# One transpose for the compressed probabilities of all heads of a step

## The chip, the cores and the metric

The kernel runs on one core of a Trainium2 chip. The metric is the time of one execution on the device, in microseconds (us), as the median of several runs. Five engines work side by side and meet at semaphores: TensorE (matmuls and transposes, into PSUM), VectorE and ScalarE (elementwise work and reductions, also out of PSUM), GpSimd (elementwise work in SBUF) and SyncE (here it issues the transfers from memory).

## The reference, cut to what matters

The whole program is two blocks over 256 tokens of width 1024. The first block has a retention layer, a sparse-attention layer and per-layer embeddings; the second has a gated delta rule, a forgetting attention and a feed-forward layer. The change lies in the sparse attention, in its compressed branch:

```python
s_c = jnp.einsum('bgrqd,bgnd->bgrqn', q, k_cmp).astype(jnp.float32) * scale
p_c = jnp.where(valid_c, jax.nn.softmax(jnp.where(valid_c, s_c, NEG), axis=-1), 0.0)
o_c = jnp.einsum('bgrqn,bgnd->bgrqd', p_c, v_cmp.astype(jnp.float32))
...
return gates[..., 0:1] * o_c + gates[..., 1:2] * o_s + gates[..., 2:3] * o_w
```

There are 16 heads in 4 groups of 4, a head is 128 wide, queries come in two blocks of 128, and there are 15 compressed keys (`CMP_N`) for each group. `v_cmp` is the result of a small two-layer network over windows of 32 tokens. With 256 tokens, the selected branch (`o_s`) and the window branch (`o_w`) are both plain causal attention.

## The kernel before, in words

All weights stream through a ring of four units of 1 MB (`ring`). ScalarE (L1461) writes each unit's high part, VectorE (L1855) what is left of it, and TensorE forms a product of two such numbers from three passes. Matmuls of plain float32 are two recorded passes each. Nearly every matmul of the program is recorded under the helper line L671.

PSUM has eight banks: four for projections and scores (`main`), four for the rest (`aux`). Each set is used in rotation in an order written out by hand. TensorE says when a bank is full, and the engine that reads it says when it is free again.

The compression network runs between the query projections. `turn_hidden` transposes its hidden values, VectorE copies them to `Pf` (L2038), `second_layer` makes the compressed keys and, in eight products, the compressed values (15 rows for each group, evicted at L2043).

The attention runs in 12 steps (`STEPS`): four with the four heads of a group for the first query block, then eight with two heads for the second. For step i:

- S: scores of the selected and the window branch; VectorE takes the maximum (L2060), ScalarE the exponential (L1627).
- N: VectorE makes the scales, GpSimd multiplies the probabilities by them (L2438).
- T (`nsa_turn`): TensorE transposes the probabilities, four times 128 x 128 for each branch (L1065), and the compressed ones, one 128 x 15 transpose for each head (L1071). VectorE copies the first (L2109), ScalarE the second (L1647), VectorE the compressed ones (L2111) to `nw`.
- O (`nsa_values`): the values' product of the three branches accumulates in one bank. The compressed one is first, contracts over 15 rows, and streams 128 columns for each head. VectorE multiplies the result by the gate (L2120); ScalarE (L1633) and VectorE (L1855) split it in two parts for the output projection.

The order on every engine is `nsa_order`: the scores of step i+2 stand between T and O of step i, and in the first three steps two gate projections stand there as well. Steps 10 and 11 have no scores left to put there.

`tab` holds constant tables: the identity (loaded first, by ScalarE's queue), masks, and tables of the second block (`TB_LEVEL`). All but the identity comes in one load, behind the first eight weight units in SyncE's queue. The tables `TB_STRICT` and `TB_INCL` aren't read.

Of the kernel before, what the change touches and what calls it, by code (L numbers as in the profile page):

```python
# [11 lines left out]
ALU = mybir.AluOpType  # L12
# [3 lines left out]
P = 128  # L16
# [91 lines left out]
SIDE_BG, SIDE_G2, SIDE_W2K, SIDE_W2V = 0, KD * 48, KD * 64, KD * 64 + 256  # L108
NSIDE = KD * 64 + 512

TB_ID, TB_CAUSAL, TB_CMP, TB_ROW, TB_STRICT, TB_INCL, TB_LEVEL = 0, 128, 256, 286, 288, 416, 544
TB_ONE = TB_LEVEL + 128 * len(LEVELS)
NTAB = TB_ONE + 15
RT_COS, RT_SIN, RT_DECAY = 0, 256, 512
# [2 lines left out]
def tables():  # L117

    i = np.arange(P)
    t = np.zeros((P, NTAB), np.float32)  # L120
    t[:, TB_ID:TB_ID + P] = np.eye(P)
    t[:, TB_CAUSAL:TB_CAUSAL + P] = np.where(i[None] <= i[:, None], 0.0, NEG)
    end = np.arange(CMP_N) * CMP_STRIDE + CMP_L - 1
    for b in range(TT):
        t[:, TB_CMP + b * CMP_N:TB_CMP + (b + 1) * CMP_N] = np.where(end[None] <= (b * P + i)[:, None], 0.0, NEG)
        t[:, TB_ROW + b] = (b * P + i >= CMP_L - 1)
    t[:, TB_STRICT:TB_STRICT + P] = np.where(i[None] < i[:, None], 0.0, -NEG)
    t[:, TB_INCL:TB_INCL + P] = np.where(i[None] >= i[:, None], 0.0, NEG)
    for n, m in enumerate(LEVELS):
        same = (i[:, None] // (2 * m)) == (i[None] // (2 * m))  # L130
        t[:, TB_LEVEL + n * P:TB_LEVEL + (n + 1) * P] = same & (i[:, None] // m % 2 == 1) & (i[None] // m % 2 == 0)
    t[:, TB_ONE + 7] = 1.0
    r = np.zeros((P, NRT), np.float32)
    inv = (np.float32(10000.0) ** (-np.arange(P, dtype=np.float32) / np.float32(P))).astype(np.float32)
    ang = (np.arange(T, dtype=np.float32)[None] * inv[:, None]).astype(np.float32)
    r[:, RT_COS:RT_COS + T] = np.cos(ang)
    r[:, RT_SIN:RT_SIN + T] = np.sin(ang)
    lg = np.log1p(-(2.0 ** (-5.0 - np.arange(RH))))
    diff = (np.arange(T)[None] - i[:, None]).astype(np.float64)
    for h in range(RH):  # L140
        r[:, RT_DECAY + h * T:RT_DECAY + (h + 1) * T] = np.where(
            diff >= 0, np.exp(np.maximum(diff, 0) * lg[h]), 0.0) * 256.0 ** -0.5
    return t, r
# [189 lines left out]
def two_models_kernel(nc, x, meta, weights, side, params, tabs, ret_tabs, p_t, gains, out):  # L333
    ctx = ExitStack()
    with ctx:
# [331 lines left out]
        def _(pe):  # L667
# [311 lines left out]
            def second_layer():  # L979

                wait_read(pe, aux, ("hT", 0))
                bank = aux.open(pe, ("c2", 0))
                for k in range(2):
                    ins = mm(bank[:, 0:CMP_ROWS], side_sb[:, SIDE_W2K + k * P:SIDE_W2K + (k + 1) * P],
                             Pf[:, k * CMP_ROWS:(k + 1) * CMP_ROWS], k == 0, k == 1)
                aux.full(ins, ("c2", 0))
                wait_read(pe, aux, ("hT", 1))
                bank = aux.open(pe, ("c2", 1))
                for g in range(NSA_G):
                    for k in range(2):  # L990
                        c0 = 2 * CMP_ROWS + k * CMP_ROWS + g * CMP_N
                        ins = mm(bank[0:CMP_N, g * P:(g + 1) * P], Pf[:, c0:c0 + CMP_N],
                                 side_sb[:, SIDE_W2V + k * P:SIDE_W2V + (k + 1) * P], k == 0, k == 1)
                aux.full(ins, ("c2", 1))

# [59 lines left out]
            def nsa_turn(i):  # L1055
                b, h0, nh = STEPS[i]
                kt = b + 1
                slot = i % 2

                pe.wait_ge(sem("nsa_p"), i + 1)  # L1060
                for key, base in ((("sT", i), 0), (("wT", i), 512)):
                    bank = aux.open(pe, key)
                    for n in range(4):
                        c0 = R2 + 2048 + slot * 1024 + base + n * P
                        ins = pe.transpose(bank[:, n * P:(n + 1) * P], R[:, c0:c0 + P], ident)  # L1065
                    aux.full(ins, key)
                pe.wait_ge(sem("cmp_p"), b + 1)
                bank = aux.open(pe, ("cT", i))
                for n in range(nh):
                    c0 = b * 240 + (h0 + n) * CMP_N  # L1070
                    ins = pe.transpose(bank[0:CMP_N, n * P:(n + 1) * P], xn[:, c0:c0 + CMP_N], ident)  # L1071
                aux.full(ins, ("cT", i))

            def nsa_values(i):
                b, h0, nh = STEPS[i]
                kt = b + 1
                slot = i % 2
                bank = aux.open(pe, ("o", i))
                for key in ("sT", "wT", "cT"):
                    wait_read(pe, aux, (key, i))  # L1080

                g = h0 // NSA_HPG
                o = bank[:, 0:nh * P]
                mm(o, Pf[0:CMP_N, CMP_V + g * P:CMP_V + (g + 1) * P], nw[0:CMP_N, slot * 512:slot * 512 + nh * P],
                   True, False)
                for br in range(2):
                    c0 = slot * 1024 + br * 512
                    p_t = PTb[:, c0:c0 + 512].rearrange("p (n k q) -> p k n q", n=nh, k=kt)
                    for k in range(kt):
                        v0 = R2 + br * 1024 + k * 512 + g * P  # L1090
                        ins = mm(o.rearrange("p (n q) -> p n q", n=nh), R[:, v0:v0 + P], p_t[:, k], False,
                                 br == 1 and k == kt - 1)
                aux.full(ins, ("o", i))
# [756 lines left out]
        def _(dve):  # L1850
# [184 lines left out]
            queries(6)  # L2035
            for n in range(2):
                bank = wait(aux, ("hT", n))
                aux.free(dve.tensor_copy(Pf[:, n * 120:(n + 1) * 120], bank[:, 0:120]), ("hT", n))  # L2038
            queries(7)
            bank = wait(aux, ("c2", 0))  # L2040
            aux.free(dve.tensor_scalar(Pf[:, CMP_K:CMP_K + CMP_ROWS], bank[:, 0:CMP_ROWS], 0.5, None, ALU.mult), ("c2", 0))
            bank = wait(aux, ("c2", 1))
            aux.free(dve.tensor_scalar(Pf[0:CMP_N, CMP_V:CMP_V + 512], bank[0:CMP_N, :], 0.5, None, ALU.mult), ("c2", 1))  # L2043
            after_read(main, ("bg", 1))
            own.then_wait(dve.tensor_scalar(bgt, bgt, 1.0, 0.5, ALU.add, ALU.mult))

# [7 lines left out]
            for kind, i in nsa_order():  # L2054
# [29 lines left out]
                elif kind == "N":  # L2084
                    b, h0, nh = STEPS[i]
                    after_read(main, ("w", i))
                    sc = esc[:, i * 8:i * 8 + 2 * nh]
                    own.then_wait(dve.reciprocal(sc, esum[:, i * 8:i * 8 + 2 * nh]))
                    g = bgt[:, b * 48 + h0 * 3:b * 48 + (h0 + nh) * 3].rearrange("p (n c) -> p c n", c=3)[:, 1:3, :]
                    sc = sc.rearrange("p (c n) -> p c n", c=2)  # L2090
                    dve.tensor_tensor(sc, sc, g, ALU.mult).then_inc(sem("nsa_scale"), 1)  # L2091
                elif kind == "G":
                    for n in (2 * i, 2 * i + 1):
                        key = ("ng", n)
                        bank = wait(main, key)
                        main.free(dve.tensor_tensor(two(R[:, R4 + n * 512:R4 + (n + 1) * 512]), two(bank), token_scale2,
                                                    ALU.mult), key)
                    for n in (2 * i, 2 * i + 1):
                        g = R[:, R4 + n * 512:R4 + (n + 1) * 512]
                        at = gates[0]  # L2100
                        gates[0] += 1
                        dve.wait_ge(sem("gate_tanh"), at + 1)
                        dve.scalar_tensor_tensor(g, tmp[:, at % 2 * 512:at % 2 * 512 + 512], 1.0, g, ALU.add,
                                                 ALU.mult).then_inc(sem("gate_ready"), 1)
                elif kind == "T":
                    b, h0, nh = STEPS[i]
                    slot = i % 2
                    bank = wait(aux, ("sT", i))
                    aux.free(dve.tensor_copy(PTb[:, slot * 1024:slot * 1024 + 512], bank), ("sT", i))  # L2109
                    bank = wait(aux, ("cT", i))  # L2110
                    aux.free(dve.tensor_copy(nw[0:CMP_N, slot * 512:slot * 512 + nh * P], bank[0:CMP_N, 0:nh * P]),  # L2111
                             ("cT", i))
                else:
                    if i:
                        attended_low(i - 1)
                    b, h0, nh = STEPS[i]
                    bank = wait(aux, ("o", i))
                    dve.wait_ge(sem("gate_ready"), (h0 + nh - 1) // 2 + 1)
                    _, y = attended_step(i)
                    aux.free(dve.scalar_tensor_tensor(y, bank[:, 0:nh * P].rearrange("p (h t) -> p h t", h=nh), 0.5, y,  # L2120
                                                      ALU.mult, ALU.mult), ("o", i))
# [426 lines left out]
```

## Time and profile before

| | |
|---|---|
| Time, median of 3 runs | 1049.89 us (1049.25 to 1051.16) |
| The profiled execution: its time | 1048.97 us |
| The profiled execution: its span, first to last instruction | 1046.6 us |
| Granted TensorE clock, mean over the span | 0.979 |
| Busy: TensorE, VectorE, ScalarE, GpSimd | 97%, 58%, 45%, 11% |
| Transfers, first two of 40 slices | 301 and 266 GB/s |
| Table load | 663.5 KB |

The span is one execution's; what lies around it is 2.4 us. A matmul's duration in the trace is from its start to its modelled end, and the next one starts before that: the distance of two starts is what one takes of TensorE's time.

### The profile page before, as it was taken

How to read it: one execution, taken by the hardware profiler on the slowest of the kernel's cores; microseconds unless marked ns; L12 is line 12 of the kernel's file. 1: busy time of each engine (PE TensorE's matmuls, PEld its weight loads, DVE VectorE, ACT ScalarE, POOL GpSimd, SP SyncE). 2: the span in 40 equal slices, each digit the busy share in tenths (PEclk: the TensorE clock that was granted, in tenths of full speed). 3: DMA queues.
4: the chain of work that ended last, by engine and by line, in shares of the span. 5: the costliest groups of instructions: out<-in, count | busy, mean ns of one | idle time of the engine just before them, and what ended most of it. 6: DMA issues, size and time to landing. Idle time of an engine off the chain costs nothing.

```text
span 1046.6 us, 15998 instructions
## 1 busy us (share of the span) xinstructions
PE 1014.1 (97%) x6484; PEld 885.1 (85%) x6484; DVE 610.6 (58%) x859; ACT 475.2 (45%) x830; POOL 113.0 (11%) x117
## 2 busy tenths in 40 slices
PE   8999999999999999999999998999999799999996
PEld 7988777879989999987787896978878689999885
DVE  4963566368856656666544779634323467576542
ACT  6334455356445434545444666332324254444332
POOL 1000120001300001013200042211200000110000
PEclk9999999999999999999999999899989899999999
DMA  8745434545556642420154442220002246555450
GB/s 301 266 135 188 161 130 177 181 174 183 177 187 245 240 159 96 147 82 1 41 189 173 161 161 92 100 92 1 1 1 81 80 166 213 170 197 189 174 201 40
DMA packets 23340, 150.54 MB, mean 144 GB/s; under 512 B 3532, under 2 KB 3800, under 8 KB 5864
## 3 DMA queue, kind: packets, MB, share of 16 engines
q1 hardware_dynamic: 22960, 149.39, 40.8%
q8 instruction: 51, 0.84, 0.3%
q10 hardware_dynamic: 312, 0.18, 0.1%
q14 instruction: 17, 0.14, 0.1%
HBM read 148.50 MB, written 1.05 MB: 143 GB/s over the span
## 4 chain that ended last, share of the span: by engine, by line
PE 91%; DVE 3%; ACT 2%; DMA 1%; issue 1%; SPq 1%; POOL 0%; ACTq 0%; POOLq 0%; DVEq 0%
PE psum L671 88%; DMA ring<-in_weights 1%; PE psum L750 1%; PE psum L1065 1%; DVE ring_parts L1855 1%; DVE R L2137 1%; ACT high_parts L1461 0%; ACT R L1468 0%; PE psum L1071 0%; PE psum L1232 0%; SPq L612 0%; DVE xT_parts L523 0%; ACT PTb L1704 0%; PE psum L1194 0%; PE psum L1236 0%
## 5 line engine op out<-in xcount | busy, mean ns | idle before, releaser
L1855 DVE TENSOR_TENSOR ring_parts<-ring,high_parts 128x1024 fp32r<-128x1024 f32 (+1 forms) x272 | 332.9, 1265 | 182.9 <-ACT high_parts L1461 182.1
L1461 ACT CAST high_parts<-ring 128x1024 fp32r<-128x1024 f32 x268 | 267.9, 1050 | 224.8 <-PE psum L671 186.8
L671 PE MATMUL psum<-xT_parts,high_parts 128*128 128x256 f32 (+1 forms) x960 | 218.0, 286 | 1.5 <-DVE ring_parts L1855 1.0
L671 PE MATMUL psum<-xT_parts,ring_parts 128*128 128x256 f32 (+1 forms) x672 | 193.0, 287 | 0.0
L671 PE MATMUL psum<-high_parts,xT_parts 128*128 128x512 f32 (+1 forms) x560 | 182.5, 403 | 6.6 <-DVE xT_parts L523 6.6
L671 PE MATMUL psum<-high_parts,R_parts 128*128 128x512 f32 (+1 forms) x560 | 167.5, 374 | 2.2 <-DVE R L2352 1.1
L671 PEld LDWEIGHTS psum<-xT_parts,high_parts 128*128 128x128 f32 x960 | 163.9, 190 | 2.6 <-DVE ring_parts L1855 1.2
L671 PE MATMUL psum<-R_parts,high_parts 128*128 128x256 f32 x832 | 160.6, 281 | 0.0
L671 PEld LDWEIGHTS psum<-high_parts,xT_parts 128*128 128x128 f32 (+1 forms) x560 | 104.3, 188 | 33.6 <-issue 8.9
L671 PEld LDWEIGHTS psum<-R_parts,high_parts 128*128 128x128 f32 x832 | 131.7, 188 | 0.1
L671 PEld LDWEIGHTS psum<-xT_parts,ring_parts 128*128 128x128 f32 x672 | 127.4, 190 | 0.1
L671 PE MATMUL psum<-ring_parts,xT_parts 128*128 128x512 f32 (+1 forms) x296 | 117.3, 396 | 0.0
L671 PEld LDWEIGHTS psum<-high_parts,R_parts 128*128 128x128 f32 (+1 forms) x560 | 99.2, 178 | 21.4 <-issue 1.3
L671 PE MATMUL psum<-ring_parts,R_parts 128*128 128x512 f32 (+1 forms) x280 | 102.0, 364 | 0.0
L671 PE MATMUL psum<-R_parts,ring_parts 128*128 128x256 f32 x352 | 98.8, 281 | 0.0
L671 PE MATMUL psum<-PTb_parts,high_parts 128*128 128x256 f32 x256 | 74.5, 291 | 0.0
L671 PEld LDWEIGHTS psum<-R_parts,ring_parts 128*128 128x128 f32 x352 | 67.5, 192 | 0.0
L671 PEld LDWEIGHTS psum<-ring_parts,xT_parts 128*128 128x128 f32 (+1 forms) x296 | 55.5, 187 | 14.0
L671 PEld LDWEIGHTS psum<-ring_parts,R_parts 128*128 128x128 f32 (+1 forms) x280 | 48.9, 175 | 9.1
L671 PE MATMUL psum<-R 128*128 128x128 f32 (+4 forms) x264 | 55.1, 341 | 0.7 <-ACT R L1807 0.7
L671 PEld LDWEIGHTS psum<-PTb_parts,high_parts 128*128 128x128 f32 x256 | 48.3, 189 | 0.0
L2438 POOL TENSOR_TENSOR R<-R,small 128x1024 f32<-128x1024 f32 x12 | 22.8, 1899 | 214.9 <-DVE small L2091 214.8
(288 smaller groups left out, 1128.0 us busy)
## 6 DMA issues: line engine op xcount, KB each, us to landing
ring<-in_weights SPq DMA_DIRECT2D x136, 1024.0 KB, 4.9
h<-in_x SPq DMA_DIRECT2D x4, 256.0 KB, 4.8
ring<-in_weights SPq DMA_DIRECT2D x4, 256.0 KB, 6.7
G<-in_gains SPq DMA_DIRECT2D x2, 512.0 KB, 7.1
out<-xn SPq DMA_DIRECT2D x2, 512.0 KB, 3.1
R<-in_ret_tabs SPq DMA_DIRECT2D x1, 768.0 KB, 12.0
tab<-in_tabs SPq DMA_DIRECT2D x1, 663.5 KB, 6.1
G<-in_p_t SPq DMA_DIRECT2D x1, 512.0 KB, 7.0
```

The source lines that it names most:

```text
L671: return pe.matmul(out, lhsT, rhs, start=first, stop=last, skip_group_check=True)
L750: ins = pe.transpose(bank[:, k * T + t * P:k * T + (t + 1) * P], src(2 * f + k, t), ident)
L1065: ins = pe.transpose(bank[:, n * P:(n + 1) * P], R[:, c0:c0 + P], ident)
L1461: act.copy(as_r(hi), value).then_inc(sem("units_high"), 1)
L1855: return dve.tensor_tensor(as_r(value), value, value_of(hi), ALU.subtract)
L2137: ins = dve.scalar_tensor_tensor(y, raw[:, j, k:k + TM], param("conv_w_2", 12 * k + j), y, ALU.mult, ALU.add)
L2438: pool.tensor_tensor(p, p, spread(esc[:, i * 8:i * 8 + 2 * nh], 1024 // (2 * nh)), ALU.mult).then_inc(sem("nsa_p"), 1)
```

## The change

In a step, the compressed probabilities of its heads lie side by side: head n has columns 15n to 15n+14. One transpose now takes them all, so that head n's keys are on partitions 15n to 15n+14, with the queries in the columns. VectorE's copy becomes a multiply: it reads the 128 columns once for each head and multiplies them by a table of ones and zeros that has a one where the partition belongs to the head. So the operand of the product has 15 x (heads) rows, and in the 128 columns of a head only that head's rows are other than zero. The compressed values are made four times over, on partitions 0 to 59: the transposed hidden values are copied four times side by side into `nw` (which isn't otherwise used then), and the eight products have 60 columns of weights. The product of the branch contracts over 60 rows (four heads) or 30 (two). The two unread tables leave `tab`, the new table of 4 columns comes in.

```diff
-TB_ID, TB_CAUSAL, TB_CMP, TB_ROW, TB_STRICT, TB_INCL, TB_LEVEL = 0, 128, 256, 286, 288, 416, 544
+TB_ID, TB_CAUSAL, TB_CMP, TB_ROW, TB_HEADS, TB_LEVEL = 0, 128, 256, 286, 288, 292
...
-    t[:, TB_STRICT:TB_STRICT + P] = np.where(i[None] < i[:, None], 0.0, -NEG)
-    t[:, TB_INCL:TB_INCL + P] = np.where(i[None] >= i[:, None], 0.0, NEG)
+    t[:, TB_HEADS:TB_HEADS + 4] = i[:, None] // CMP_N == np.arange(4)[None]
...
-                        c0 = 2 * CMP_ROWS + k * CMP_ROWS + g * CMP_N
-                        ins = mm(bank[0:CMP_N, g * P:(g + 1) * P], Pf[:, c0:c0 + CMP_N],
+                        c0 = (k * NSA_G + g) * 4 * CMP_N
+                        ins = mm(bank[0:4 * CMP_N, g * P:(g + 1) * P], nw[:, c0:c0 + 4 * CMP_N],
                                  side_sb[:, SIDE_W2V + k * P:SIDE_W2V + (k + 1) * P], k == 0, k == 1)
...
-                for n in range(nh):
-                    c0 = b * 240 + (h0 + n) * CMP_N
-                    ins = pe.transpose(bank[0:CMP_N, n * P:(n + 1) * P], xn[:, c0:c0 + CMP_N], ident)
-                aux.full(ins, ("cT", i))
+                c0 = b * 240 + h0 * CMP_N
+                aux.full(pe.transpose(bank[0:nh * CMP_N, 0:P], xn[:, c0:c0 + nh * CMP_N], ident), ("cT", i))
...
-                mm(o, Pf[0:CMP_N, CMP_V + g * P:CMP_V + (g + 1) * P], nw[0:CMP_N, slot * 512:slot * 512 + nh * P],
+                m = nh * CMP_N
+                mm(o, Pf[0:m, CMP_V + g * P:CMP_V + (g + 1) * P], nw[0:m, slot * 512:slot * 512 + nh * P],
                    True, False)
...
-                aux.free(dve.tensor_copy(Pf[:, n * 120:(n + 1) * 120], bank[:, 0:120]), ("hT", n))
+                if n == 0:
+                    aux.free(dve.tensor_copy(Pf[:, 0:120], bank[:, 0:120]), ("hT", n))
+                else:
+                    four_times = nw[:, 0:480].rearrange("p (g n c) -> p g n c", g=8, n=4)
+                    once = bank[:, 0:120].rearrange("p (g c) -> p g c", g=8)
+                    aux.free(dve.tensor_copy(four_times, once.unsqueeze(2).to_broadcast([P, 8, 4, CMP_N])), ("hT", n))
...
-            aux.free(dve.tensor_scalar(Pf[0:CMP_N, CMP_V:CMP_V + 512], bank[0:CMP_N, :], 0.5, None, ALU.mult), ("c2", 1))
+            aux.free(dve.tensor_scalar(Pf[0:4 * CMP_N, CMP_V:CMP_V + 512], bank[0:4 * CMP_N, :], 0.5, None, ALU.mult), ("c2", 1))
...
-                    aux.free(dve.tensor_copy(nw[0:CMP_N, slot * 512:slot * 512 + nh * P], bank[0:CMP_N, 0:nh * P]),
-                             ("cT", i))
+                    m = nh * CMP_N
+                    apart = nw[0:m, slot * 512:slot * 512 + nh * P].rearrange("p (h q) -> p h q", h=nh)
+                    aux.free(dve.tensor_tensor(apart, over(bank[0:m, 0:P], nh), spread(tab[0:m, TB_HEADS:TB_HEADS + nh], P),
+                                               ALU.mult), ("cT", i))
```

`over` repeats an operand for each head, `spread` repeats each of its columns.

## Rows read from the trace of the kernel before

**Rows 1.** The page: the chain that ended last, by engine.

```profile
PE 91%; DVE 3%; ACT 2%; DMA 1%; issue 1%; SPq 1%; POOL 0%; ACTq 0%; POOLq 0%; DVEq 0%
```

**Rows 2.** The same chain in order of time: start us, us, what.

```profile
59.14 93.59 PE psum L671 x392
...
433.60 0.44 PE psum L1071 x4
...
481.61 0.22 PE psum L1071 x2
...
510.80 0.41 DVE nw L2111
...
515.68 46.55 PE psum L671 x202
...
594.59 2.55 ACT R L1468 x8
```

**Rows 3.** Line L1071: durations ns min/median/max, first and last start, forms.

```profile
L1071 PE MATMUL psum<-tab,xn x32: 272/272/273, 415.3 to 514.8; 128*15 128x128 f32 x32
```

**Rows 4.** Timeline, TensorE's weight loads (PEld): start us, us, what, [idle before].

```profile
433.32 0.42 PEld L1071 LDWEIGHTS psum<-tab,xn 128*15 128x15 f32 x4
433.76 0.19 PEld L671 LDWEIGHTS psum<-xT_parts,high_parts 128*128 128x128 f32 x1
...
478.12 0.29 PEld L671 LDWEIGHTS psum<-nw,Pf 15*128 15x128 f32 x2 [0.27 <-issue]
478.74 1.59 PEld L671 LDWEIGHTS psum<-PTb,R 128*128 128x128 f32 x8 [0.33 <-issue]
...
481.34 0.20 PEld L1071 LDWEIGHTS psum<-tab,xn 128*15 128x15 f32 x2
481.56 0.30 PEld L671 LDWEIGHTS psum<-R 128*128 128x128 f32 x2
...
483.88 0.29 PEld L671 LDWEIGHTS psum<-nw,Pf 15*128 15x128 f32 x2 [0.27 <-issue]
```

**Rows 5.** Lines of VectorE at the steps, and the timeline at steps 4 and 10.

```profile
L2109 DVE COPY PTb<-psum x12: 683/685/692, 419.2 to 514.4; 128x512 f32<-128x512 f32 x12
L2111 DVE COPY nw<-psum x12: 400/402/668, 419.8 to 515.1; 15x256 f32<-15x256 f32 x8, 15x512 f32<-15x512 f32 x4
L2120 DVE SCALAR_TENSOR_TENSOR R<-psum,R x12: 424/425/693, 432.8 to 518.3; 128x256 f32<-128x256 f32 x8, 128x512 f32<-128x512 f32 x4
...
476.50 0.40 DVE L2111 COPY nw<-psum 15x256 f32<-15x256 f32 x1
...
510.25 0.38 PE L1071 MATMUL psum<-tab,xn 128*15 128x128 f32 x2
```

**Rows 6.** Timeline, weight loads in the later forgetting attention.

```profile
720.74 0.29 PEld L671 LDWEIGHTS psum<-R 64*128 64x128 f32 x2
721.18 0.29 PEld L671 LDWEIGHTS psum<-R,tab 8*128 8x128 f32 x2
721.61 0.10 PEld L671 LDWEIGHTS psum<-causal_b,ident_b 128*128 128x128 bf16 x1
```

**Rows 7.** Timeline, weight loads at the end of the first compression layer.

```profile
376.07 0.13 PEld L671 LDWEIGHTS psum<-ring_parts,R_parts 128*60 128x60 f32 x1
376.19 0.19 PEld L671 LDWEIGHTS psum<-xT_parts,high_parts 128*128 128x128 f32 x1
```

**Rows 8.** Timeline around the second compression layer.

```profile
382.74 0.46 DVE L2038 COPY Pf<-psum 128x120 f32<-128x120 f32 x2
...
383.97 2.36 DVE L1855 TENSOR_TENSOR ring_parts<-ring,high_parts 128x1024 fp32r<-128x1024 f32 x2 [0.77 <-ACT high_parts L1461]
...
390.48 0.30 PEld L671 LDWEIGHTS psum<-R 128*128 128x128 f32 x2 [0.21 <-issue]
```

**Rows 9.** Windows: stretch, us, busy (x instructions) of PE, PEld, DVE, ACT, POOL, clock, DMA share, GB/s.

```profile
480.30:503.30 23.00, 23.00 (x130) 17.67 (x129) 13.23 (x32) 12.15 (x40) 7.59 (x4) 1.00 0.00 1
```

**Rows 10.** Windows, a stretch of 5 us of the second block.

```profile
705.00:710.00 5.00, 5.00 (x16) 3.08 (x16) 1.88 (x4) 0.41 (x3) 0.00 (x0) 0.50 0.00 0
```

## Prediction

> **What bounds the kernel now.** I read the page first: TensorE makes 91% of the chain that ended last [rows 1], VectorE 3%. That share says little about one stage, so next I read that chain in order of time, to see through which engine the stage under change is passed [rows 2]. Between 430 us and 509 us every piece of it is TensorE, with the transposes of the probabilities (L1065), those of the compressed probabilities (L1071) and everything recorded under the helper line L671 following each other without a gap. Only at about 510 us and again 4 us later does it leave TensorE: at the last two steps (10 and 11) there are no scores of a later step to compute, and the chain goes through three VectorE instructions, L2120, L2109 and last the copy of the transposed compressed probabilities (L2111, at 510.80 us the first time). From 515.7 us it is TensorE again, until ScalarE's squares at 594.6 us. Then I read the stage instruction by instruction [rows 3, 4] to get a price for one transpose that is a distance between starts, not the duration of one (272 ns [rows 3]): these overlap, and the duration would overprice it by a factor of two and a half.
>
> **What the change removes.** Per step, the transposes of the compressed probabilities: four become one in the four steps of four heads, two become one in the eight steps of two heads. In a step of two heads the two weight loads start at 481.34 us and the next kind of work at 481.56 us [rows 4], so one costs 0.11 us. In a step of four heads, four loads start at 433.32 us and the next work at 433.76 us [rows 4]: again 0.11 us. The chain says the same, 0.44 us for four and 0.22 us for two [rows 2].
> - Four steps, three transposes less each: 4 x 3 x 0.11 = 1.32 us. Nothing else ends there: the chain is TensorE's before and after.
> - Steps 4 to 9, one less each: 6 x 0.11 = 0.66 us. The copy of the compressed values for the product at 478.12 us was issued at 476.50 us and took 0.40 us [rows 5], so it was done 1.2 us ahead of its reader. TensorE isn't waiting for it, and gets all of what its own queue loses.
> - Steps 10 and 11, one less each: nothing. The product waits for L2111, which stands behind L2109 and L2120 on VectorE [rows 2, 5], and L2109 begins after the other step's product was read. The transposes removed here end while L2109 is still running (they start at 510.25 us, 0.38 us for both, so 510.63 us [rows 5]; L2111 can't start before VectorE is through with L2109, at 510.80 us [rows 2]). TensorE then waits 0.11 us longer for the same moment.
>
> Sum removed: 1.98 us of 2.20 us.
>
> **What it adds.** (1) L2111 turns from a copy into a multiply whose table operand is broadcast: 60 or 30 partitions, same 512 or 256 columns. No row shows that instruction. Below, the copy itself: 0.668 us at 512 and 0.40 us at 256 [rows 5]. Above, the nearest with PSUM and an SBUF operand: L2120 at 0.693 us and 0.425 us [rows 5]. I take the upper end, +0.02 us. In ten steps the 1.2 us of slack covers it; in steps 10 and 11 it is on the chain: 2 x 0.02 = 0.04 us. If the cover were gone everywhere it would be 12 x 0.02 = 0.24 us.
>
> (2) The product of the compressed branch contracts over 60 or 30 rows in place of 15, with the same streamed columns. Two passes of 256 columns took from 478.12 us to 478.74 us [rows 4], of which the columns themselves are about 0.43 us (in the same step eight weight loads with such passes, 128 rows each, spread over 1.59 us, 0.20 us from one to the next) and about 0.2 us is a gap before the next weight load. Would 60 rows widen that gap? The later attention of this kernel has products over 64 rows next to products over 8 rows of equal width: the pair over 64 rows took 0.44 us to the next start and the pair over 8 rows 0.43 us, before a load of 128 rows [rows 6]. The gap is there in both and equal. Zero, with 0.01 us x 4 as its upper end.
>
> (3) The transpose itself now has 60 or 30 columns of weights in place of 15. Loads of 60 columns in the compression layer follow each other every 0.12 us, and so does the load of 128 columns after them [rows 7]. Priced at zero against the 15-column one.
>
> (4) The eight products that make the compressed values (16 weight loads of 15 columns) have 60 columns of weights each, same number, same streamed 128 columns: zero by the same rows of 60 columns. Their eviction on VectorE covers 60 partitions, not 15, at the same 512 columns; time follows columns (the copies of 15 partitions and of 128 partitions, 512 columns each, took 0.668 us and 0.685 us [rows 5]), so +0.02 us at most, and the first product that waits for it comes after eight score products of other heads.
>
> (5) The second of the two copies at 382.74 us (0.23 us each) becomes one of 480 columns, about 0.65 us by the 512-column copy: +0.4 us on VectorE [rows 5, 8]. Behind it is queued the split of a weight unit (L1855), which found VectorE idle for 0.77 us waiting for ScalarE [rows 8], so it isn't moved. Its reader on TensorE, the second compression layer, comes a whole query projection later (48 products). Without the cover it would cost 0.4 us, once.
>
> (6) The table loses 252 columns, 126 KB of one load that SyncE issues behind the first eight weight units. The units behind it are used from 59.14 us on, and from there the chain is TensorE alone for 93.59 us [rows 2], so the shorter transfer is hidden: zero. Had a unit been late, the gain would be at most 126 KB at the page's 266 GB/s of that slice, about 0.5 us.
>
> **Total.** 0.04 - 1.98 = -1.94 us. The profiled execution took 1048.97 us (span 1046.6 us and 2.4 us around it), which becomes 1047.0 us; the profiled execution stands 0.9 us below the median of the runs shown. Against that median, 1049.89 - 1.94 = 1047.95 us: -0.18%. About 0.2% (2.1 us) is what a measurement can tell from no change, so the forecast is just on the near side of what shows.
>
> Does the gain survive? The stream of weights idles through the steps (DMA share 0.00 from 480 us to 503 us [rows 9]): the ring is full, so nothing that must arrive sets the pace, and what follows at 515.7 us is bound by TensorE to 594 us [rows 2]. After that the chain passes through ScalarE and VectorE, but each of its pieces depends on the one before, not on a clock of its own, so the shift goes to the end.
>
> **Rivals.**
> - *The single transpose pays a change of shape* (the slower side). On leaving the products with 15 columns of weights, TensorE's weight queue showed 0.21 us of idle before the next load [rows 8], and one appears around the narrow-row product too [rows 4]. If the one wide transpose, between full-size transposes and scores, got such a gap on both sides, that is 0.4 us x 12 = 4.8 us, net +2.9 us: 1052.8 us. It decides from 1.94 / 12 = 0.16 us per step. Against it: the 15-column transposes, which differ more from the 128 columns around them, have no gap at all (loads every 0.11 us straight through [rows 4]), and the 60-column loads have none either. The Trainium skill (TensorEngine Tiling, Tiling Modes, Key Properties) says that changing the tiling mode, not just the tile, drains TensorE, and it lists configurations of 32, 64 and 128 columns. By that rule 15 and 60 columns both differ from the 128 around them: if it holds for transposes, both pay alike and the forecast stands; this rival is the case in which only the wide one pays. The trace shows no drain at the 15-column transposes. Chance 0.07.
> - *The shift is absorbed later*: some step after 594 us waits for something that the sparse attention doesn't delay. 1049.9 us. For it: there the chain changes engine many times. Against: no piece of it near 594 us is a transfer. Chance 0.14.
> - *More is gained*: TensorE also saves sequencer work (fewer instructions and waits in a queue that shows idle "issue" before the product, 0.27 us a step [rows 4]). If a third of that gap went in ten steps, 0.9 us more: 1047.0 us. Chance 0.11.
> - *The clock decides*: from 640 us to 825 us the granted clock falls several times from its upper level of 2.4 GHz to 1.2 GHz (its mean is 0.50 from 705 us to 710 us [rows 10]), and a shift by 2 us can lay one more or one fewer there. Such a stretch of 5 us loses up to 2.5 us of TensorE work; the three runs of before lie 1.9 us apart, which is about one. 1046 us or 1050 us. Chance 0.10.
>
> **How the numbers follow.** The forecast keeps 0.58, its own range 1047.0 to 1048.9 us (the 1.9 us between runs, about it). The range reaches up past the absorbed case's middle to 1049.9 us and down to 1046.3 us (more gained, or a clock stretch less). Faster by more than 0.2% needs under 1047.8 us: 0.45 of the forecast's chance (its centre is 0.15 us short of the line), most of "more is gained", half of the clock's: 0.26 + 0.09 + 0.05 = 0.40. Slower by more than 0.2%: the change of shape, 0.07, and a little of the clock's: 0.08. Same: 0.52.
>
> **What would show it.** In the changed profile, 12 transposes at the place of L1071 and not 32; a step of two heads that repeats every 5.65 us and not 5.76 us (478.12 us to 483.88 us is one product to the next [rows 4]); no new gap between transpose and scores; the multiply at 0.67 to 0.70 us and 0.40 to 0.43 us; TensorE's wait for VectorE in the last two steps a little longer, about 0.8 us each. The prediction is wrong if the 60-row product or the single transpose has a wider gap than its predecessor, if the multiply takes over 1.2 us more than the copy, or if the end of the attention comes 2 us earlier and the end of the span doesn't.

## The result and the profile after

The changed kernel took 1051.05 us (median of 22 runs) and the kernel before 1048.44 us (22 runs); the ratio is 1.0029 [1.0017 to 1.0042]. It became slower, by 2.6 us in the medians and 3.0 us by the ratio, where 1.9 us less was forecast. (A ratio, here and below, comes with its 95% interval. It is not the quotient of the two medians, from which it differs by up to 0.16%.) The profiled executions took 1050.09 us (span 1048.3) after and 1048.97 us before.

The edited stage itself did what was forecast. First the profile's view of the two new lines (durations ns min/median/max, first and last start us, forms):

```profile
L1069 PE MATMUL psum<-tab,xn x12: 272/272/273, 416.4 to 513.9; 128*30 128x128 f32 x8, 128*60 128x128 f32 x4
L2116 DVE TENSOR_TENSOR nw<-psum,tab x12: 401/402/674, 420.9 to 514.3; 30x256 f32<-30x256 f32 x8, 60x512 f32<-60x512 f32 x4
```

There are 12 transposes instead of 32 [rows 3], and the multiply costs what the copy cost, to 6 ns [rows 5]. Next, TensorE's weight loads in the timeline of after, a step of four heads and one of two (start us, us, what, idle before):

```profile
471.85 0.29 PEld L670 LDWEIGHTS psum<-nw,Pf 60*128 60x128 f32 x2 [0.26 <-issue]
472.90 0.30 PEld L670 LDWEIGHTS psum<-PTb,R 128*128 128x128 f32 x2 [0.76 <-issue]
...
477.92 0.29 PEld L670 LDWEIGHTS psum<-nw,Pf 30*128 30x128 f32 x2 [0.26 <-issue]
478.54 1.59 PEld L670 LDWEIGHTS psum<-PTb,R 128*128 128x128 f32 x8 [0.33 <-issue]
480.16 1.01 PEld L1064 LDWEIGHTS psum<-tab,R 128*128 128x128 f32 x8
481.14 0.10 PEld L1069 LDWEIGHTS psum<-tab,xn 128*30 128x30 f32 x1
481.25 0.30 PEld L670 LDWEIGHTS psum<-R 128*128 128x128 f32 x2
...
483.57 0.29 PEld L670 LDWEIGHTS psum<-nw,Pf 30*128 30x128 f32 x2 [0.26 <-issue]
```

The step repeats every 483.57 - 477.92 = 5.65 us (5.76 before [rows 4]). The wide transpose hands over after 0.11 us, with no gap. The product over 30 rows holds its place for 0.62 us, as the one over 15 rows did [rows 4].

So the time went elsewhere. The chain of waits in order of time lays the two executions side by side; the pieces below have the same instructions in both. Of before, as far as not shown [rows 2]:

```profile
29.89 28.66 PE psum L671 x240
...
179.41 33.22 PE psum L671 x144
...
248.05 134.04 PE psum L671 x1052
...
382.48 32.07 PE psum L671 x276
...
854.16 121.81 PE psum L671 x1036
...
977.04 60.69 PE psum L671 x264
```

Of after:

```profile
29.37 28.80 PE psum L670 x240
...
58.77 93.89 PE psum L670 x392
...
179.60 33.84 PE psum L670 x144
...
248.98 134.26 PE psum L670 x1052
...
383.63 32.11 PE psum L670 x276
...
514.94 47.39 PE psum L670 x202
...
853.92 122.58 PE psum L670 x1036
...
977.58 61.85 PE psum L670 x264
```

The sparse attention, from the start of x276 to the start of x202, went from 515.68 - 382.48 = 133.20 us to 514.94 - 383.63 = 131.31 us: -1.89 us, against -1.94 forecast. But it began 1.15 us later, and from the start of x1036 to the end of x264 it is 1.94 us more (183.57 to 185.51 us). The middle, from the start of x202 to the start of x1036, took 0.50 us more. 1.15 - 1.89 + 0.50 + 1.94 = 1.70 us, the difference of the spans. Every long stretch of dense products but x276 is longer, by 0.2% to 1.9%, though nothing in it was edited and TensorE waits for nothing in it. With the smaller pieces (x96 +0.26, x80 +0.07, x48 +0.04) these stretches add 4.4 us; -1.9 + 4.4 = +2.5 us, near the 2.6 us between the medians. The two profiled executions differ by less, 1.70 us, because in this one of after the first stretch began 0.52 us earlier, and the middle, apart from what x202 and x80 lost, took about 0.4 us less.

One product shows the size. TensorE's products in the timeline (R is the weights, 512 columns are streamed from the ring or `high`), after:

```profile
530.43 0.40 PE L670 MATMUL psum<-ring_parts,R_parts 128*128 128x512 f32 x1
...
531.83 0.40 PE L670 MATMUL psum<-ring_parts,R_parts 128*128 128x512 f32 x1
```

From one ring product to the next are three products (another one starts at 531.13 us); six take 531.83 - 530.43 = 1.40 us here, 233 ns each. In before six took 1.38 us (ring products at 530.25 and 531.63 us), 230 ns each. Over the whole of x202 the difference is 0.84 / 202 = 4 ns for each product.

Do the other engines or the transfers slow these products? In the last stretch, x264, all of them are idle for over 8 us. The row of windows in after (stretch, us, busy and instructions of PE, PEld, DVE, ACT, POOL, granted clock, DMA share, GB/s):

```profile
1026.50:1035.20 8.70, 8.70 (x39) 7.00 (x38) 0.00 (x0) 0.00 (x0) 0.00 (x0) 1.00 0.00 0
```

TensorE's products there, in after:

```profile
1027.12 0.40 PE L670 MATMUL psum<-ring_parts,R_parts 128*128 128x512 f32 x1
...
1034.82 0.39 PE L670 MATMUL psum<-ring_parts,R_parts 128*128 128x512 f32 x1
```

and in before, where they are idle from 1025.10 us to 1033.60 us:

```profile
1025.66 0.39 PE L671 MATMUL psum<-ring_parts,R_parts 128*128 128x512 f32 x1
...
1033.21 0.39 PE L671 MATMUL psum<-ring_parts,R_parts 128*128 128x512 f32 x1
```

Every third product streams from the ring, so this is 33 products, in 7.70 us against 7.55 us, 233.3 ns against 228.8 ns each. The 4 to 5 ns are there while TensorE works alone.

### The profile page after: what moved, and what is told of

The parts are those of the page before. It is cut to its first block, busy times and chain, and to the rows that moved or that the text cites. A ratio compares the mean times of both kernels' runs of the same rounds, so it can differ in the third digit from the quotient of the medians.

```text
span 1048.3 us, 15958 instructions
## 1 busy us (share of the span) xinstructions
PE 1015.3 (97%) x6464; PEld 882.4 (84%) x6464; DVE 609.2 (58%) x859; ACT 474.8 (45%) x830; POOL 112.5 (11%) x117
## 3 DMA queue, kind: packets, MB, share of 16 engines
HBM read 148.37 MB, written 1.05 MB: 143 GB/s over the span
## 4 chain that ended last, share of the span: by engine, by line
PE 92%; DVE 3%; ACT 2%; DMA 1%; issue 1%; POOL 0%; SPq 0%; ACTq 0%; POOLq 0%; DVEq 0%
PE psum L670 88%; PE psum L749 1%; PE psum L1064 1%; DVE ring_parts L1853 1%; DVE R L2142 1%; DMA ring<-in_weights 1%; DMA h<-in_x 1%; PE psum L1230 0%; ACT R L1466 0%; DVE xT_parts L522 0%; ACT high_parts L1459 0%; PE psum L1234 0%; ACT PTb L1702 0%; PE psum L1192 0%; POOL small L2379 0%
```

## Experiments

**Old places.** The changed kernel with an unused buffer of 992 bytes behind `tab`:

```diff
         tab = sb("tab", NTAB)
+        sb("gap", 248)
```

> The changed kernel with an unused buffer of 248 columns behind the tables, so that par, h, xn, xT, R, PTb and all behind them lie at the very addresses that they had before the change. Theory P (the places of the buffers): the attention keeps its gain of 1.9 us and the rest runs as before: 1.9 us faster than the kernel before, ratio about 0.998; products of TensorE with R as weights start every 226 to 230 us thousandths (0.226 to 0.230 us) again, not every 0.234 us. Rival E (the edit in the attention costs later on, by a clock stretch or a wait): as slow as the changed kernel, +2.6 to +3.0 us, ratio about 1.003.

1046.68 us (12 runs) against 1048.92 us for before (29 runs), ratio 0.9974 [0.9955 to 0.9993]. Its chain:

```profile
179.77 33.21 PE psum L671 x144
...
382.84 32.10 PE psum L671 x276
...
513.98 46.56 PE psum L671 x202
...
973.95 60.69 PE psum L671 x264
```

The stretches are those of before to 0.03 us (x1052: 134.04 us in both), and the gain of the edit stands: 513.98 - 382.84 = 131.14 us of attention, 2.06 us less than before. So 0.17 us of what the attention lost to the places is hidden in the 1.89 us of the changed kernel. It was run once more, with nothing changed, beside later ones:

> e1 once more, for its ratio: 1.9 us faster than before, ratio 0.998; every stretch of the chain outside the second block within 0.1 us of e1.

1045.64 us (12 runs) against 1047.27 us, ratio 0.9978 [0.9957 to 0.9998].

**The other half alone.** The kernel before, with only the unread tables out of `tab`, so that it has 1203 columns as in the changed kernel and the buffers lie exactly as there (the expectation counted 1199 columns and 1024 bytes, which was a slip):

```diff
-TB_ID, TB_CAUSAL, TB_CMP, TB_ROW, TB_STRICT, TB_INCL, TB_LEVEL = 0, 128, 256, 286, 288, 416, 544
+TB_ID, TB_CAUSAL, TB_CMP, TB_ROW, TB_LEVEL = 0, 128, 256, 286, 292
...
-    t[:, TB_STRICT:TB_STRICT + P] = np.where(i[None] < i[:, None], 0.0, -NEG)
-    t[:, TB_INCL:TB_INCL + P] = np.where(i[None] >= i[:, None], 0.0, NEG)
```

> The kernel before with only the two unread tables left out (1199 columns of tables, so 1024 bytes less, the buffers behind them lie nearly as in the changed kernel). Theory P: slower than before by what the changed kernel lost outside the attention, +4.5 us, ratio about 1.004. Rival E: no difference from before (0.0 us, ratio 1.000); the transfer that is 128 KB shorter would give at most 0.5 us.

1054.31 us (8 runs), ratio 1.0050 [1.0032 to 1.0067]: +0.50%, without any edit of the attention. Its chain has the stretches of after (x1036 too, 122.57 us):

```profile
516.76 47.39 PE psum L669 x202
...
982.95 61.85 PE psum L669 x264
```

The two halves add up: -0.26% and +0.50% make +0.24%, and the whole measured +0.29%. The rival falls: the loss comes without the edit of the attention, and goes while the edit stays.

**How far, and of what?** Two kernels with 32 bytes more: the changed one with `sb("gap", 8)` behind `tab`, and before with the same.

> The changed kernel with 8 unused columns (32 bytes) behind the tables: the buffers lie 32 bytes from where the change put them and 960 bytes from where they were before, but start at a multiple of 64 again. Theory P in the form 'a start that is no multiple of 64 bytes costs': 1.9 us faster than before, ratio 0.998. Theory P in the form 'the absolute place counts': as the changed kernel, ratio 1.003. Rival E: as the changed kernel too.

> The kernel before with 8 unused columns (32 bytes) behind the tables: nothing else changes, every buffer behind them starts at 32 above a multiple of 64 bytes. Theory P in the form 'a start that is no multiple of 64 bytes costs': +4.5 us, ratio 1.004. In the form 'the absolute place counts', and by rival E: within 1 us of before.

The second was as slow as with the short table, as the form "a start that is no multiple of 64 bytes costs" has it (1053.46 us, 10 runs; ratio 1.0050 [1.0035 to 1.0066]). The first matched no form of what was expected: 1048.94 us (12 runs), ratio 1.0010 [0.9992 to 1.0029], with some stretches shorter than in any kernel so far and others longer (x1052 134.67 us, and x1036):

```profile
178.82 32.89 PE psum L671 x144
...
513.77 46.14 PE psum L671 x202
...
854.93 124.27 PE psum L671 x1036
...
980.28 60.14 PE psum L671 x264
```

x144, x202 and x264 have R as weights, x1036 streams R (256 columns). One and the same place was the best of all that were tried for the one and the worst for the other.

**One buffer, or all together.** The kernel with old places, and in it either everything 32 bytes higher (`sb("front", 8)` ahead of the ring) or R and what is behind it alone (`sb("gap2", 8)` ahead of R).

> As e1 (the changed kernel, buffers at their places of before), with 8 unused columns in front of the first buffer as well: now every buffer, ring and high too, starts at 32 above a multiple of 64 bytes, and the distances between them are those of before. If what counts is how two operands of a product lie to each other: as e1, 1.9 us faster than before, the x202 stretch of the output projection 46.5 us. If each buffer's own start counts: slower than e1 by at least what the changed kernel lost, 4.5 us, the same stretch 47.4 us or more.

> As e1, with 8 unused columns between xT2 and R: h, xn, xT, xT2 lie as before the change, R and all behind it start at 32 above a multiple of 64 bytes. If R's place carries the loss: the x202 stretch 47.4 us and the last x264 stretch 61.8 us as in the changed kernel, the first x240 and x392 stretches (xT is their operand) 28.66 us and 93.6 us as before; about 3.5 of the 4.5 us lost, so 1.5 to 2 us slower than before. If h, xn or xT carry it: as e1.

Everything shifted together: stretch for stretch the old times (33.22, 134.04, 46.57, 60.69 us); 1046.11 us (10 runs), ratio 0.9994 [0.9975 to 1.0012]. This interval holds both no change and the 0.2% that was expected; it is the stretches that tell. R shifted alone:

```profile
30.12 28.66 PE psum L672 x240
...
515.03 47.38 PE psum L672 x202
...
975.04 61.85 PE psum L672 x264
```

1049.14 us (10 runs), ratio 1.0018 [1.0002 to 1.0034]. The stretches with R are slow (x1036 too, 122.56 us) and x240, whose operands are xT and the ring, is not. So it isn't a buffer's own place that counts but its distance to the buffer of the other operand. Of the 4.4 us that the stretches lose between old and new places, R carries about 3.8.

**Which distances.** Three more kernels: the changed one with `sb("gap", 24)` (96 bytes more); then, from the one with old places, `front` 8 with `gap` 256 (R itself at a multiple of 128 bytes, its distance that of the changed kernel); `gap` 120 (all behind `tab` 512 bytes below the old places). The last two have one execution each (1051.39 and 1049.01 us), and only their stretches are used.

> The changed kernel with 24 unused columns (96 bytes) behind the tables: the buffers start at 64 above a multiple of 128 bytes, as before the change, and 896 bytes lower than then. If the start within 128 bytes is all that counts: stretch for stretch as e1 (x202 46.56 us, x1036 121.8 us, x264 60.69 us), 1.9 us faster than before. If the absolute place counts: unlike e1.

> As e1, with ring, high and the tables 32 bytes higher (8 unused columns in front) and everything behind the tables 64 bytes higher (8 more behind them). R then starts at a multiple of 128 bytes as in e3 and e8, but lies 32 bytes off its old distance from the weight buffers, as in the changed kernel. If the distance of the operands counts: the changed kernel's stretches, x144 33.84 us, x202 47.39 us, x264 61.85 us, x392 93.89 us. If R's own start counts: those of e8, 32.9, 46.15 and 60.1 us. Its one time tells nothing at this size.

> As e1, with every buffer behind the tables 512 bytes lower than there (a gap of 120 columns, not 248). If the distance of two operands counts only modulo 512 bytes or less: stretch for stretch as e1 (x144 33.21 us, x202 46.56 us, x264 60.69 us, x1052 134.04 us). If its period is 1024 bytes (e3 and e8, 1024 bytes apart, agree within 0.04 us where R is the weights): unlike e1.

The distance R - `high` modulo 512 bytes (worked out from the declarations) and the pieces of the chain, in us:

```
kernel                    mod 512   x240    x144   x1052   x202   x1036   x264
before                      448    28.66   33.22  134.04  46.55  121.81  60.69
old places                  448    28.66   33.21  134.04  46.56     *    60.69
old places again            448      *     33.22  134.04  46.57  121.81  60.69
all shifted by 32           448    28.66   33.22  134.04  46.57     *    60.69
512 bytes lower             448    28.66   33.21  134.04  46.56  121.81  60.70
after                       480    28.80   33.84  134.26  47.39  122.58  61.85
before, short table         480      *     33.84  134.26  47.39  122.57  61.85
before, 32 more             480    28.79   33.84  134.26  47.39  122.57  61.85
only R 32 more              480    28.66   33.83  134.23  47.38  122.56  61.85
R at 128, distance as after 480    28.79   33.84  134.26  47.38  122.58  61.85
after, 32 more                0    28.63   32.89  134.67  46.14  124.27  60.14
after, 96 more               64    28.64   33.84  134.51  47.38  122.01  61.85
* the chain of that execution is cut elsewhere, so this piece has another length
```

Kernels of one distance agree to 0.03 us, whatever else differs in them. No two distances agree in all columns, though some agree in one: 480 and 64 have the same x144, x202 and x264, and differ in x1052 and x1036. (x240 goes by xT's distance, which is that of R in all of them but "only R 32 more", where it is still 448.) 512 bytes lower is no change. 448 and 64 differ by 128 bytes and in x144 by 0.63 us, so the period is not 128; between 256 and 512 these runs don't decide. The kernel with 96 bytes more took 1050.80 us (6 runs), ratio 1.0047 [1.0028 to 1.0065]. Its stretches (x96 and x48 included) add up to 3.5 us over the old places, 3.7 us with the attention. By the ratios it is some 7 us slower than the kernel with old places, by the medians against before some 5 us: the rest is not explained.

**Is there a better place than the old one?** Of the four distances tried, R as weights is fastest at 0, R as the streamed operand at 448. First R moved up 64 bytes (with `into_ffn` 64 more); then also the parts of R that are streamed (`into_ffn`, and `into_kv`'s low half) set back by 64 bytes. The second, on top of the kernel with old places:

```diff
+        sb("gap2", 16)
         R = sb("R", 4 * 4096, True)
+        sb("gap3", 16)
...
-            return kt_cols(xT, kt, M, T), R[:, R4 + kt * T:R4 + (kt + 1) * T]
+            return kt_cols(xT, kt, M, T), R[:, R4 - 16 + kt * T:R4 - 16 + (kt + 1) * T]
...
-            return R[:, R4 + kt * T:R4 + (kt + 1) * T], R[:, R4 + 2048 + kt * T:R4 + 2048 + (kt + 1) * T]
+            c0 = R4 - 16 + kt * T
+            return R[:, c0:c0 + T], R[:, c0 + 2048:c0 + 2048 + T]
```

> As e1, with R at a multiple of 128 bytes (16 unused columns in front of it), and only the input of the feed-forward layer, which TensorE streams from R, kept at 64 above one (16 columns further in R, which is 16 columns longer). By the stretches of e3: x202 46.14 us (0.4 less than e1), x264 60.14 us (0.55 less), x144 32.9 us (0.3 less), and x1036 121.8 us and not 124.3 us. About 1.3 us faster than e1, 3 us faster than before, ratio 0.997. Rival: the place of what is streamed matters elsewhere too, and the gain is lost between 248 and 382 us (134.7 us and not 134.0 us).

> As e1, with R at a multiple of 128 bytes (16 unused columns in front of it, 16 behind), and both inputs that TensorE streams from its last quarter (the low parts for the key and value projection, the input of the feed-forward layer) 16 columns lower, so at the very distance from the weight buffers that they had before. The stretches in which R is the weights as in e8 (x144 32.9 us, x202 46.15 us, x264 60.1 us), the streams as in e1 (x1052 134.1 to 134.3 us where e8 had 134.40, x1036 121.8 us where e8 had 122.01). Sum of the stretches against e1 -1.3 us, against before -3.2 us, ratio 0.997.

The first: x1052 134.40, x1036 122.01, x264 60.12 us, 0.6 us less than old places over all stretches, where 1.3 us was expected; 1047.40 us (12 runs), ratio 1.0003 [0.9984 to 1.0021]: no gain in the timing. The second:

```profile
178.84 32.93 PE psum L674 x144
...
247.20 134.11 PE psum L674 x1052
...
512.99 46.13 PE psum L674 x202
...
854.25 121.81 PE psum L674 x1036
...
977.13 60.12 PE psum L674 x264
```

Both demands are met. The stretches take 1.3 us less than with the old places, and the attention 0.15 us more, so 1.1 us are left; 1045.68 us (12 runs) against 1047.27 us, ratio 0.9979 [0.9962 to 0.9995]. The same kernel with old places, timed beside it, had 0.9978: what the stretches show is below what this timing can tell. Either is about 0.2% faster than the kernel before, and so about 0.5% faster than the changed one, beside which neither was timed.

**Why the timing tells so little.** The 24 runs of the old-places kernel lie between 1041.25 and 1049.69 us. Its two profiled executions (identical work, first fence the first one) show where. The chain from ScalarE's squares to the last block's transposes:

```profile
592.88 2.55 ACT R L1467 x8
...
843.81 0.87 PE psum L750 x8
```

```profile
592.03 2.55 ACT R L1467 x8
...
846.21 0.87 PE psum L750 x8
```

250.93 us and 254.18 us: 3.25 us apart between two executions of one program. The rows of windows (stretch, us, busy and instructions of each engine, granted clock, DMA share, GB/s) for most of it:

```profile
643.00:846.00 203.00, 192.82 (x1218) 159.68 (x1217) 90.70 (x159) 75.49 (x172) 24.74 (x28) 0.92 0.17 58
```

```profile
643.00:846.00 203.00, 192.83 (x1203) 158.89 (x1202) 85.73 (x155) 73.10 (x167) 24.99 (x28) 0.90 0.16 54
```

The longer one had the lower mean clock there. The granted clock is 0.50, which is 1.2 GHz, in parts of this stage [rows 10], and these do not lie at the same times: from 770 to 775 us the first execution has a mean of 0.50 and the second 0.68, from 780 to 785 us 0.71 and 0.50.

## Why the prediction was wrong, point by point

- **What bounds the kernel**: right, and more than was drawn from it. If 91% of the chain is TensorE [rows 1], a change of 1% in the time from one product to the next is worth more than the whole edit.
- **What the change removes**: right. 0.11 us per transpose, ten steps gain, steps 10 and 11 don't. The attention became 1.89 us shorter (2.06 us with the old places); forecast 1.94.
- **(1) the multiply**: 0.674 and 0.402 us, 0.006 us over the copy at most; 0.02 was taken. Right.
- **(2) 60 and 30 rows**: right. 30 rows hold 0.62 us. 60 rows go from 471.85 to 472.90 us, 1.05 us, the same as 15 rows did in the step of four heads.
- **(3), (4) 60 columns of weights**: right; there is no gap around the wide transpose, and x276 with the second compression layer in it changed by 0.04 us.
- **(5) the copy of 480 columns**: 0.65 us as forecast, and hidden.
- **(6) the table loses 252 columns**: this is the step that failed. It asked only what the shorter transfer saves and answered zero. The transfer is one effect of a shorter table; the other is that every buffer behind it moves by 992 bytes against those ahead of it. That costs 4.4 us by the stretches, more than twice what the edit gains. It was isolated by the short table in the kernel before (+0.50%) and by the changed kernel with old places (-0.26%). No rival of the prediction has it either.
- **Does the gain survive**: yes. With the old places the kernel is 0.26% and 0.22% faster, and 0.06% with everything shifted together, where the operands have the same distances. The mean of the three is -0.18%, the forecast. That it is so exact is luck, as each interval is about 0.2% to either side.
- **Rivals.** *The single transpose pays a change of shape* gave 1052.8 us, near the measured time, by a mechanism that isn't there: 481.14 us transpose, 481.25 us next load. A time that fits is no proof of its reason. *Absorbed later* and *the clock decides* weren't the cause either: with the old places the gain is there, and in after the stretches x240 to x1052, x202, x1036 and x264 have a granted clock of 1.00. *More is gained*: the idle "issue" before the product stayed 0.26 us (0.27 before [rows 4]).
- **Steps 10 and 11**: TensorE's waits for the other engines, in the view of waits of after:

```profile
PE psum L670 <- DVE nw L2116: 0.8, 1, 0.8
```

0.8 us where 0.7 was the longest before: 0.1 more, as forecast. It is one wait, at step 10. The wait at step 11, 0.8 us too, is put down to ScalarE's copy of the other probabilities (L1645), which ended at 514.69 us, the multiply at 514.67 us: a tie, where the forecast had the multiply last.

## What to carry to other kernels

```profile
1028.45 0.39 PE L671 MATMUL psum<-ring_parts,R_parts 128*128 128x512 f32 x1
...
1035.93 0.39 PE L671 MATMUL psum<-ring_parts,R_parts 128*128 128x512 f32 x1
```

1035.93 - 1028.45 = 7.48 us for 33. Over the whole of x202, in which the others work too, the three are 230.4, 234.6 and 228.4 ns. With R streamed, 256 columns, x1036 divided by its products gives 117.6 ns at 448, 117.8 at 64, 118.3 at 480 and 120.0 at 0. So with R as the weights the loss is TensorE's own, between buffers that it streams and buffers that it loads as weights. That reads of the streamed operand and of the next weights hinder each other in the memory is an argument and not shown; the dependence on the distance is. The Trainium skill (TensorE: Matmul & The Clock Gate, Part 2) says that TensorE has two independent SBUF read ports and that loading the next tile's weights doesn't steal read bandwidth from the running matmul. If that is meant for every placement of the two buffers, these runs don't bear it out, though they don't show which accesses meet: between the slowest and the fastest distance tried, a stretch differs by 0.5% (x1052) to 3% (x144).

Left open: whether the period is 256 or 512 bytes, what the distances between those tried do, and why the kernel with 96 bytes more took longer than its stretches explain.
